# Expert rows gathered for four pairs at a time from two float32r parts, in place

## What is computed

```python
scores = jax.nn.sigmoid(xf @ w_router)             # (256, 64)
# group-limited choice of 8 experts a token, weights normalised to 2.5
y = sum over chosen e of w_e * (silu(xf @ w_gate[e]) * (xf @ w_up[e])) @ w_down[e]
x = layer_norm(alpha * x + y + shared_swiglu(xf), ln2_g, ln2_b)
```

## Time and profile before

| | us |
|---|---|
| three timed runs | 1202.4, 1202.93, 1203.32 (median 1202.93) |
| the profiled execution | 1203.37 |
| its span, first to last instruction | 1201.5 |

### The profile page before, as it was taken

The page is one execution under the profiler, slowest core; times in us unless marked ns, Lnnn a source line. Parts: engine busy times, 40 slices in busy tenths (PEclk is TensorE's granted clock), DMA queues, the critical chain, the costliest instruction groups (busy, mean ns, idle before and its releaser), DMA issues.

```text
span 1201.5 us, 17935 instructions
## 1 busy us (share of the span) xinstructions
PE 1175.7 (98%) x7776; PEld 553.0 (46%) x7776; DVE 347.0 (29%) x1057; ACT 261.9 (22%) x513; POOL 10.4 (1%) x20
## 2 busy tenths in 40 slices
PE   7999999999999999999999999999999999999995
PEld 6764534444444434444386655344444443443431
DVE  0434722222222222222343346222222222222214
ACT  1132321222212222111112323221222211212110
POOL 0000000000000000000000000000000000000001
PEclk9999999999999999999999999999999999999998
DMA  9972599999999999999987625999999999999991
GB/s 386 422 300 116 210 387 429 426 428 427 427 427 428 427 427 427 427 427 426 422 353 305 238 95 229 417 426 428 428 426 427 427 427 427 426 428 427 428 427 77
DMA packets 36070, 452.41 MB, mean 377 GB/s; under 512 B 3984, under 2 KB 4112, under 8 KB 6928
## 3 DMA queue, kind: packets, MB, share of 16 engines
q1 hardware_dynamic: 35984, 451.18, 89.6%
HBM read 450.12 MB, written 1.05 MB: 376 GB/s over the span
## 4 chain that ended last, share of the span: by engine, by line
PE 92%; DMA 4%; DVE 3%; issue 1%; ACT 0%; POOL 0%; POOLq 0%; DVEq 0%
PE bank L638 36%; PE bank L670 18%; PE bank L537 8%; PE bank L571 6%; PE bank L816 5%; PE bank L744 5%; DMA slots<-in_w_gu 3%; PE bank L753 2%; PE bank L652 2%; PE bank L594 1%; PE bank L763 1%; PE bank L773 1%; PE bank L556 1%; PE bank L849 1%; PE bank L699 1%; PE bank L703 1%
## 5 line engine op out<-in xcount | busy, mean ns | idle before, releaser
L670 PE MATMUL bank<-slots,low 128*32 128x512 f32 x2048 | 233.0, 595 | 1.1 <-issue 1.1
L638 PE MATMUL bank<-slots,low 128*64 128x512 f32 x1024 | 226.5, 594 | 0.2 <-DMA slots<-in_w_gu 0.2
L638 PE MATMUL bank<-slots,xT 128*64 128x512 f32 x1024 | 226.1, 594 | 0.0
L1279 DVE SCALAR_TENSOR_TENSOR yparts<-bank,small,yparts 128x512 fp32r<-128x512 f32 x128 | 96.0, 750 | 271.1 <-ACT yparts L976 271.1
L976 ACT ACTIVATE yparts<-bank,small 128x512 fp32r<-128x512 f32 x128 | 88.0, 687 | 241.8 <-PE bank L670 241.8
L638 PEld LDWEIGHTS bank<-slots,low 128*64 128x64 f32 x1024 | 69.3, 137 | 133.0 <-issue 130.8
L638 PEld LDWEIGHTS bank<-slots,xT 128*64 128x64 f32 x1024 | 69.4, 137 | 132.2 <-issue 132.2
L1271 DVE TENSOR_TENSOR high<-high,bank 128x256 f32<-128x256 f32 x64 | 26.9, 421 | 339.7 <-ACT high L1004 339.7
L670 PEld LDWEIGHTS bank<-slots,low 128*32 128x32 f32 x2048 | 60.4, 109 | 138.8 <-issue 138.8
L537 PEld LDWEIGHTS bank<-high,low 128*128 128x128 bf16 x1536 | 100.0, 147 | 48.7 <-issue 48.7
L1004 ACT ACTIVATE high<-bank 128x256 f32<-128x256 f32 x64 | 24.6, 385 | 425.6 <-PE bank L638 425.6
(11 more groups left out here) (126 smaller groups left out, 659.7 us busy)
## 6 DMA issues: line engine op xcount, KB each, us to landing
slots<-in_w_gu SPq DMA_DIRECT2D x128, 2048.0 KB, 25.4
slots<-in_w_dn SPq DMA_DIRECT2D x64, 2048.0 KB, 24.6
slots<-in_dense SPq DMA_DIRECT2D x30, 1024.0 KB, 14.8
slots<-in_first SPq DMA_DIRECT2D x4, 768.0 KB, 7.9
r<-in_pool_mat SPq DMA_DIRECT2D x2, 1024.0 KB, 22.4
r<-in_ln_g SPq DMA_DIRECT2D x4, 512.0 KB, 4.6
r<-in_ln_b SPq DMA_DIRECT2D x4, 512.0 KB, 5.9
sdn<-in_shared_dn SPq DMA_DIRECT2D x2, 1024.0 KB, 9.7
```

The costliest lines, as they stand in the source:

```text
L638: m = pe.matmul(H[64 * a:64 * a + 64, :], xg[B % 2][:, k, j, a, :], GU[g][:, a, :, k, :], start=k == 0, stop=k == KD - 1)
L670: m = pe.matmul(Y[half][r0:r0 + 32, :], hT[:, kc * P + 64 * a + 32 * t:kc * P + 64 * a + 32 * t + 32], DN[g][:, a, kc, half * 512:(half + ...
L1279: dve.scalar_tensor_tensor(ysp[:, 1, half * 512:(half + 1) * 512], Y[half][:, :], wslot[:, b:b + 1], ysp[:, 0, half * 512:(half + 1) * 512 ...
```

## The change

A block is now four pairs (`SPAN = 4`): eight experts, 256 columns of slots. x is split into two float32r parts instead of three bfloat16 ones, written chunk by chunk (a chunk's 128 columns lie side by side). One chunk of a block's gather is 2 token tiles x 2 parts = 4 matmuls of 256 columns, and a pair carries two chunks. The gathered rows have one buffer of 32 cells (`cells`) in place of two: each pair's chunks go into the cells that the pair has just read, in an order that rotates from block to block (`cell`, `cells_of`). It covers `xT` and the part of `low` behind it, so nothing can be loaded into `xT` before the pass's last `h_full`.

`sel` is needed in float32r for the gather and in bfloat16 (`selb`) for `turn_sel`; DVE builds both, once in four pairs. The first block's eight chunks use banks 4, 5, 6, 7, 2, 1, 6, 7. The shared expert's second transposition moves from before pair 0 to behind pair 0's gather. The second norm's gains move from `r8` to weight buffer 1, loaded when the last pair has read its first half (`last_norms`); in layer 1 these two transfers of 512 KB stand between the first and second halves of `memt` and chunk 0, and all of these wait for the last pair's `h_full`.

```diff
+SPAN = 4
+BLOCKS = PAIRS // SPAN
+FIRST_BANKS = (4, 5, 6, 7, 2, 1, 6, 7)
...
+        cells = front[:, 0:2 * KD * S].rearrange("p (c e s) -> p c e s", e=2, s=64)
+        def cell(B, k, j):
+            return sum(1 << (b + 2 * B) % 5 for b in range(5) if SPAN * k + j >> b & 1)
+        def by_chunk(v, chunked):
+            return v.rearrange("p (k r) -> p k r", k=KD) if chunked else v.rearrange("p (r k) -> p k r", k=KD)
+        def cells_of(B, k):
+            v = front[:, 0:2 * KD * S].rearrange("p (a b c d e w) -> p a b c d e w", a=2, b=2, c=2, d=2, e=2)
+            at, r = cell(B, k, 0), 2 * B % 5
+            ix = [slice(None) if b in (r, (r + 1) % 5) else at >> b & 1 for b in range(4, -1, -1)]
+            return v[(slice(None), *ix, slice(None))], r == 4
...
+            def last_norms(l):
+                sp.wait_ge(main.h_half, (l + 1) * PAIRS)
+                norms(l, 1)
...
-                    sp.wait_ge(main.h_full, last + 1)
+                    sp.wait_ge(main.h_full, l * PAIRS)
...
                     sp.dma_start(r[:, a:z], dense[l, 0][:, a:z]).then_inc(chunk_in[0][h], 16)
+                    if h == 0:
+                        last_norms(l - 1)
...
-                sp.wait_ge(*x_at(l, 0, NT - 1))
-                norms(l, ln2_g, ln2_b)
...
-            def gather(ps, quarter, buf, to):
-                for kk in range(2):
-                    for t in range(NT):
-                        m = gather_rows(kk, t, quarter, buf, to)
+            def gather(ps, k, to):
+                for t in range(NT):
+                    for s in range(2):
+                        m = pe.matmul(to[:].rearrange("p (x t c) -> p x t c", x=2 * SPAN, t=NT)[:, :, t, :],
+                                      xsp[:, t, s, k * P:(k + 1) * P], sel[:, t, :].rearrange("p (x c) -> p x c", x=2 * SPAN),
+                                      start=s == 0, stop=s == 1)
                 m.then_inc(ps.g_full, 1)
...
+                for k in range(KD):
                     if round_ is None:
+                        to = bank[FIRST_BANKS[k]]
...
+                        if k >= 6:
+                            pe.wait_ge(ps.g_sb, first_fill + k - 3)
...
+                    gather(ps, k, to)
                 if round_ is None:
-                    shared_turn(l, 1)
                     pe.wait_ge(w3_rd, l + 1)
...
+                    if first and round_ is None:
+                        shared_turn(l, 1)
                     pe.wait_ge(ps.h_rd, n + 1)
...
+                def g_out(B, k, src):
+                    act.wait_ge(ps.g_full, first_fill + KD * B + k + 1)
+                    dst, crossed = cells_of(B, k)
+                    order = "p (a b w) -> p b a w" if crossed else "p (a b w) -> p a b w"
+                    copy(dst, src[:].rearrange(order, a=2, b=2)).then_inc(ps.g_sb, 1)
...
+                def split(t):
+                    act.wait_ge(*x_at(l, 0, t))
+                    copy(by_chunk(xsp[:, t, 0, :], 1), by_chunk(xs[:, t, :], 0)).then_inc(split_hi, 1)
...
+            def split_low(l, t):
+                dve.wait_ge(split_hi, 2 * l + t + 1)
+                dve.tensor_tensor(by_chunk(xsp[:, t, 1, :], 1), by_chunk(xs[:, t, :], 0), by_chunk(xsp[:, t, 0, :].bitcast(F32), 1), ALU.subtract).then_inc(split_rd, 1)
...
                 def build_sel(B):
+                    for to, done in ((sel, ps.sel_rd), (selb[:, B % 2], ps.selb_rd)):
+                        for t in range(NT):
+                            m = dve.tensor_tensor(to[:, t, :].rearrange("p (e c) -> p e c", e=wide), slots,
...
+                        m.then_inc(done, 1)
...
-                split_residual(l, 1)
+                split_low(l, 1)
                 choose(1)
```

More of the change, by code:

```diff
@@ L165, in build @@
         xs = sb("xs", [P, NT, D])
-        xT = sb("xT", [P, KD, S])
         cst = sb("cst", [P, NCONST])
+        with nc.sbuf_tensor("selr", [P, NT * SPAN * 64], F32R) as selr:
+            pass
         r8 = sb("r8", [P, 2048])
@@ L173, in build @@
         power = sb("power", [P, 1])
-        low = sb("low", [P, YS_AT])
+        with nc.sbuf_tensor("cells_at", [P, 2 * KD * S], F32), nc.sbuf_tensor("xparts", [P, NT * 2 * D], F32R) as xparts:
+            pass
+        front = sb("front", [P, KD * S + YS_AT])
+        xT = front[:, 0:KD * S].rearrange("p (k s) -> p k s", k=KD)
+        low = front[:, KD * S:]
         with nc.sbuf_tensor("yparts", [P, 2 * D + 2 * P], F32R) as yparts:
@@ L210, in build @@
         off[0] = 0
[L211 to L217, removed]
+        xsp = xparts[:].rearrange("p (t s d) -> p t s d", t=NT, s=2)
+        off[0] = YS_AT
         off[0] += 2 * D + 2 * P
@@ L220, in build @@
         sg = part(2 * F).rearrange("p (t n) -> p t n", t=NT)
-        sel = part(2 * NT * P // 2, BF16).rearrange("p (b t c) -> p b t c", b=2, t=NT)
         pos = part(NT * E)
-        off[0] = NT * 3 * D // 2 + D + KD * 2 * P
+        sel = selr[:].rearrange("p (t c) -> p t c", t=NT)
+        selb = r8[:, NT * SPAN * 64:2 * NT * SPAN * 64].bitcast(BF16).rearrange("p (b t c) -> p b t c", b=2, t=NT)
+        hT = r8[:, D:D + 2 * F]
+        w3 = r8[:, D + 2 * F:D + 2 * F + NT * E * 3 // 2].bitcast(BF16).rearrange("p (t e s) -> p t e s", t=NT, s=3)
+        off[0] = YS_AT
         sig = part(NT * E)
@@ L1004, in body @@
                     act.activation(sg[:, 0, :], H[:, 0:F], ACT.Silu).then_inc(ps.silu_rd, 1)
-                    if q // 2 + 1 < BLOCKS:
-                        for f in range(2):
-                            g_quarter(q // 2 + 1, 2 * (q % 2) + f, Y[f])
+                    B, j = q // SPAN, q % SPAN
+                    if B + 1 < BLOCKS:
+                        for i in range(2):
+                            g_out(B + 1, 2 * j + i, Y[i])
+                    if first and round_ is None:
+                        shared_turned(l, 1)
                     act.wait_ge(ps.selT_sb, n + 1)
@@ L1257, in run @@
                 if round_ is None:
-                    split_last(l, 1)
                     weights(l, 0)
@@ L1265, in body @@
                 def body(n, q, g, b, use, first, last):
-                    if q % 2 == 0 and q // 2 + 1 < BLOCKS:
+                    if q % SPAN == 0 and q // SPAN + 1 < BLOCKS:
+                        dve.wait_ge(ps.g_full, KD * (turn * BLOCKS + q // SPAN + 1))
                         if not first:
                             dve.wait_ge(ps.selT_ps, n)
-                        build_sel(q // 2 + 1)
+                        build_sel(q // SPAN + 1)
                     dve.wait_ge(ps.silu_rd, n + 1)
@@ L1379, in _ @@
                 half_stats(l, 1, 0, "wo2")
-                split_residual(l, 0)
-                split_last(l, 0)
+                split_low(l, 0)
                 def choose(t):
```

110 lines of the change are left out of this document (42 added, 68 removed).

## The result

The changed kernel takes 1209.31 us (median of 4 runs, 1206.5 to 1210.53), the kernel before 1203.12 beside it (4 runs, 1202.4 to 1203.34): a ratio of 1.005, 95% interval 1.0038 to 1.0062. It is slower by 6.2 us, above the forecast of 1203.1 and outside its range. The profiled execution took 1209.54 us, its span 1207.7.

The account below looks back on a forecast made before the run. Loads (14.73 us a pair) were taken to bind before pair 27, PE (PE's own 13.74) after. Terms +0.35 - 2.42 + 3.3 + 1.0 + 0.35 - 2.42 = +0.2 us gave a median of 1203.1 us, range 1199.5 to 1207.

Parts of the forecast that it names:

- The page's 92% of PE: PE's share of the chain; the rival that PE alone binds claimed 28 us faster, 1175 us, chance 0.04.
- Between the layers: Layer change: PE stalls in kmT for late second halves, +3.3 us (1.8 to 3.4), and the clock may fall, +1.0.
- The clock: Half clock after the layer-change stall: +1.0 us taken, bounds 0 and 3.2; rival with the whole 3.2, 1205.3 us, chance 0.25.
- The split: Ahead of pair 0: DVE reading x at a step of eight floats was taken to cost nothing.
- Its rival's price: Rival that the strided split is slower: +1.2 us a layer from double time, 1205.5 us, chance 0.10.
- The first gather: Before pair 0: 32 matmuls at 0.115 us and turn_sel, 3.8 us for 3.44, so +0.35 us a layer.
- Pairs 27 to 31: End of each pass: less gather work on PE, -2.42 us in each layer, with no new wait taking it back.
- The cover: Pairs before 27: PE's slack against loads, claimed lost only if the gather cost over 0.99 us a pair more.
- the rival with slow matmuls: Gather matmuls at float32's 0.22 us: 4.1 us more a layer, 1211 us, chance 0.05.

Follow-up runs that it names:

- the loads are cut: Both kernels with only the first half of the down weights loaded from pair 3 on: old kernel 1202.04 us, changed kernel 1182.02 us.
- the run with spare matmuls: Changed kernel with ten spare float32 matmuls in the gap of the keys (kmT), loads still late: 1205.59 us, ratio 1.0028.
- The kernel before with the late loads: Kernel before, with first dense chunk and memt waiting for pair 31's H and 1 MB of gains between the chunk's halves: 1210.05 us, ratio 1.0058.
- the split side by side: Changed kernel with the split written and read side by side, the gather's stationary operand read at a step of eight floats: 1240.69 us, ratio 1.0318.
- the early chunk alone: Changed kernel with dense chunk 0 issued behind pair 29 again, memt and then the norm gains behind the last H: 1201.54 us, ratio 0.9989.
- the fastest version: Changed kernel with early dense chunk, second tile's subtraction behind the first row selection, shared expert's down projection in pairs 4 to 7: 1197.26 us, ratio 0.9955.
- the two losses mended: Changed kernel with early dense chunk and the second tile's low-part subtraction moved on VectorE behind the first row selection: 1198.88 us, ratio 0.9964.

## Why the prediction was wrong

Its picture of the passes was right. The period is 13.25 us (forecast 13.2), PE meets the loads at pair 19 in both layers (18), each H then lasts 1.4 us longer (some 1.5) at 427 GB/s, and 27 pairs' gain in two layers is worth nothing until the loads are cut, when the changed kernel is 20 us ahead. The page's 92% of PE was right that PE bound the old kernel, where less to load changed nothing, and said nothing of what a faster PE would gain.

What failed is the sizes around the passes.

- **Between the layers: +4.3 forecast, +7.0 measured.** The step is "Between the layers", both of its terms. The stall was there, behind the eighth record and for the dense chunk, as written, but lasted 4.8 us (8 records at the old pace take 1.75, and 595.45 + 1.75 to 601.96 is 4.76) and not 3.3. The second half landed 14.4 us behind memt's issue instead of 13.1. (H of pair 31 ended 1.0 us later than forecast, but that moved the issue and PE alike.) The term that was too small is the gains. By their 1.05 MB at 427 GB/s they were to take 2.5 us; in the trace they landed 3.7 us behind chunk 0's first half (594.49 to 598.16), while what stood ahead of them and behind them took what the forecast gave it (6.9 us for 7.1, 3.8 for 3.7). The run that moves them out of the way agrees: its gap is 3.6 us shorter. While they moved, the rate was low (the last two columns are DMA share and GB/s):

```profile
596.00:597.00 1.00, 1.00 (x6) 0.90 (x5) 1.00 (x3) 0.00 (x0) 0.00 (x0) 1.00 1.21 266
597.50:598.00 0.50, 0.00 (x0) 0.00 (x0) 0.50 (x1) 0.00 (x0) 0.00 (x0) 1.00 0.70 262
```

With the gains last it dipped later, to 291 GB/s from 599 to 600. They are rows of 4 KB, each copied to all 128 partitions; whether that is why they are slow is not shown. The clock cost 2.2 us and not 1.0, and the run with spare matmuls shows it alone. The forecast had 3.2 as the upper bound and chose low on the ground that "little is idle beyond those 2 us"; a longer stall takes that ground away. The kernel before with the late loads shows the whole term in an old kernel: 7.5 us.
- **The split: nothing forecast, 1.1 us a layer measured.** "Loads on PE at that step take 191 ns, side by side 192, so I take nothing" was the wrong row: a weight load of float32 says nothing about VectorE or ScalarE. With x read at a step of eight floats they took 2.01 us for 1.23 and 2.07 for 1.06. Even on PE the row holds for float32 only, since float32r loads went from 188 to 338 ns. The rule that the prediction set aside, in the Trainium skill's "SBUF — State Buffer", section Specifications (TRN2), that full bandwidth takes two hits on a 16-byte line, was right for both engines. Its rival's price, 1.2 us a layer, was met in part by luck: it was worked out from double time, and the subtraction grew by 0.78. With the split side by side PE still waits 0.50 us for the counting where it waited 0.17, and where these 0.3 us come from is open. What made the step cost time was its place: moved behind the selection, the same 2.01 us cost nothing.
- **The first gather: +0.35 forecast, +0.56 measured** from the counting to pair 0 (7.29 us before, 7.85 now): 0.124 us a matmul, not 0.115.
- **Pairs 27 to 31: -2.42 forecast, -1.27 and -1.05 measured.** From the end of H of pair 27 to that of pair 31 the changed kernel saves 2.4 us in both layers (62.0 to 59.6), and with the loads cut it is 2.3, so PE's part was sized well. What took the other half back is that pair 27's loads came late. In the changed kernel one H about pair 25 waits longer in each layer:

```profile
494.85 3.65 PE L663 MATMUL bank<-slots,front 128*64 128x512 f32 x16 [2.74 <-DMA slots<-in_w_gu]
...
1093.49 5.35 PE L663 MATMUL bank<-slots,front 128*64 128x512 f32 x16 [2.84 <-DMA slots<-in_w_gu]
```

In layer 1 the clock fell as well, 5.35 us for 16 records of 3.65. H of pair 27 ended 378.4 and 378.9 us behind pair 0's start (377.3 and 377.5 before). With the early chunk alone it ended at 376.8 and 377.0. That long wait sits at other pairs in other runs (at pair 22 with the early chunk, at pair 31 in the fastest version) and is small or absent in some layers. So how much of this term a run keeps is in part chance. Why one transfer comes late is open: DMA moves 423 GB/s from 480 to 495 us and 428 on either side.
- **The cover.** "The cover goes only if the gather cost more than 0.99 us a pair above the old one" was a slip. Loads and PE were level at pair 27, so nothing covers a slower PE. It changed no number of the sum, but with the gather at a step it was wrong by 25 us, and the 1211 of the rival with slow matmuls left out some 12 us (54 pairs, 8 x 0.22 for 1.53 us).

Two of these terms were each named as a rival, the clock at 0.25 and the split at 0.10, and priced one at a time. The split's came true almost in full (1.1 of 1.2 us a layer) and the clock's by two thirds (2.2 of 3.2), at once and on top of a longer stall.

With the two losses mended the change is worth what it frees outside the loads: 1198.88 us, 4.0 under the kernel before.

## What to carry to other kernels

Where loads and compute end level, a gain on compute inside the loop is worth nothing and a loss counts in full, so price both signs separately, and look for the gain at the ends, where one of them has slack. When a buffer is made to serve longer, ask first which load now waits for it and what is queued behind that load: here this cost more than all else. Moving 1 MB that nobody was waiting for from the middle of that queue to its end mended most of it, and sending one chunk early, into a buffer that was free anyway, the rest. Price a strided access by a row of the same engine and type, and ask what stands behind it in that engine's order before moving it to another engine.

## What the runs showed of the hardware

- At a step of eight floats a VectorE subtraction of 128x1024 float32 took 2.01 us for 1.23, and a ScalarE copy 2.07 for 1.06.
- Float32r weight loads of 128 columns at a step of eight floats: 338 ns against 188. Float32 ones: 191 against 192.
- The granted clock fell from full to half in a stall of 4.8 us, with PE idle since 597.4 and the fall between 599.5 and 600.0, and came back near 606.5, some 4.5 us after PE had resumed at 601.96. A stall of 0.91 us left it at full. Of the seven waits of 2.5 to 2.9 us in the middle of an H, over all runs, four were followed by the half clock (2.54, 2.75, 2.78, 2.84) and three were not (2.56, 2.74, 2.80). After the wait of 2.84 us it fell only when PE had been at work again for some 1.1 us.
- While GpSimd subtracted 1024 float32 columns (2.85 us), a VectorE instruction of 64 columns lasted 2.42 us, 2.75 in layer 1, instead of 0.20; another, just ahead of it and also within GpSimd's time, took its usual 0.21.
- 1.05 MB of gains took 3.6 to 3.7 us of a queue that moves 427 GB/s otherwise, where their bytes ask for 2.5.
